# A one-core decoder step: the cached keys of each sample transposed in 32x32 blocks on VectorE and scored by sixteen 32x32 tiles of TensorE

## What is computed

```python
s_past = einsum('nqhd,nkhd->nhqk', q, k_past) * ATTN_SCALE + cq - c_past   # k_past: 2048 x 16 x 64
s_new  = einsum('nqhd,nkhd->nhqk', q, k_new)  * ATTN_SCALE + cq - c_new    # causal among the 4 new rows
p = softmax(concatenate([s_past, s_new]))
out = p[past] @ v_past + p[new] @ v_new
```

## Time and profile before

| what | us |
|---|---|
| median of 3 runs (lowest, highest) | 1737.45 (1736.69, 1746.53) |
| span of the profiled execution | 1738.2 |
| TensorE busy in the span | 1580.9 (91%) |
| one iteration of the attention loop | 62.0 |
| attention, first key transpose to second projection tile | 721.4 to 1250.0 |

### The profile page before, as it was taken

One profiled execution on the slowest core, in us unless ns is written; L12 is line 12 of the kernel. 1 busy time (PEld: TensorE's weight loads), 2 busy tenths in 40 slices (PEclk: granted clock), 3 DMA queues, 4 the chain that ended last, 5 costly groups with the idle time before them and its releaser, 6 DMA issues.

```text
span 1738.2 us, 23311 instructions
## 1 busy us (share of the span) xinstructions
PE 1580.9 (91%) x7920; PEld 864.2 (50%) x7920; DVE 484.5 (28%) x1110; ACT 339.2 (20%) x696; POOL 120.1 (7%) x176
## 2 busy tenths in 40 slices
PE   4999999999849999599999999999995999999992
PEld 4874444444424444265656555555444444444440
DVE  3330000000032232355555554555124100000002
ACT  2120000000111111333333333433210000000010
POOL 1020000000020000100001010010000300000002
PEclk8899999999969999789999999999995999999996
DMA  8279888888871131558988898888623588888755
GB/s 247 105 247 338 330 336 333 334 332 322 300 251 37 49 97 49 189 182 269 300 299 288 288 298 285 297 301 295 246 115 122 153 333 335 334 336 338 321 217 184
DMA packets 115110, 435.78 MB, mean 251 GB/s; under 512 B 26823, under 2 KB 44296, under 8 KB 102511
## 3 DMA queue, kind: packets, MB, share of 16 engines
q1 hardware_dynamic: 85111, 370.75, 59.0%
q0 software_dynamic: 11472, 33.92, 6.1%
q10 hardware_dynamic: 18480, 30.48, 4.8%
HBM read 397.90 MB, written 37.58 MB: 251 GB/s over the span
## 4 chain that ended last, share of the span: by engine, by line
PE 73%; issue 12%; SPq 4%; DVE 3%; DMA 3%; ACT 3%; POOL 1%; ACTq 0%; DVEq 0%; POOLq 0%
PE PS L839 24%; PE PS L857 12%; PE PS L938 10%; PE PS L1079 6%; PE PS L1145 3%; PE PS L1097 3%; PE PS L1063 3%; PE PS L780 3%; PE PS L1024 2%; SPq L460 2%; PE PS L1044 1%; SPq L386 1%; DMA KB<-yd,SLi 1%; PE PS L847 1%; PE PS L1127 1%
## 5 line engine op out<-in xcount | busy, mean ns | idle before, releaser
L839 PE MATMUL PS<-W,VB 128*128 128x512 f32 x1024 | 454.7, 598 | 9.7 <-DVE VB L1572 5.5
L839 PEld LDWEIGHTS PS<-W,VB 128*128 128x128 f32 x1024 | 194.1, 192 | 242.2 <-issue 230.7
L857 PE MATMUL PS<-W,VB 128*128 128x512 f32 x512 | 226.9, 596 | 4.2 <-ACT VB L1295 4.2
L1722 DVE TENSOR_TENSOR VB<-VB,PS 128x512 f32<-128x512 f32 x32 | 22.0, 688 | 617.5 <-PE PS L839 617.5
L1079 PE MATMUL PS<-C,KB 128*128 128x128 f32 x1024 | 167.9, 295 | 12.4 <-ACT W L1458 10.8
L1079 PEld LDWEIGHTS PS<-C,KB 128*128 128x128 f32 x1024 | 117.5, 147 | 78.3 <-issue 59.4
L857 PEld LDWEIGHTS PS<-W,VB 128*128 128x128 f32 x512 | 95.7, 192 | 113.7 <-issue 109.1
L1301 ACT ACTIVATE VB<-PS 128x1024 f32<-128x1024 f32 x32 | 32.7, 1023 | 436.1 <-PE PS L857 436.1
L1458 ACT ACTIVATE W<-PS 128x512 f32<-128x512 f32 x128 | 76.1, 594 | 170.2 <-PE PS L1079 161.6
L1900 DVE COPY W<-PS 128x512 f32<-128x512 f32 x128 | 88.0, 688 | 65.5 <-PE PS L1079 63.7
L1097 PE MATMUL PS<-W 128*32 128x256 f32 x1024 | 84.3, 402 | 2.9 <-DVE W L1995 1.4
(11 more groups left out here) (255 smaller groups left out, 1454.0 us busy)
## 6 DMA issues: line engine op xcount, KB each, us to landing
W<-in_w_gate SPq DMA_DIRECT2D x32, 2048.0 KB, 13.3
W<-in_w_up SPq DMA_DIRECT2D x32, 2048.0 KB, 17.7
W<-in_w_down SPq DMA_DIRECT2D x32, 2048.0 KB, 8.7
KB<-in_cache_k SPq DMA_DIRECT2D x128, 512.0 KB, 5.3
W<-in_cache_v SPq DMA_DIRECT2D x64, 512.0 KB, 5.6
VB<-in_cache_v SPq DMA_DIRECT2D x64, 512.0 KB, 7.3
yd<-VB ACTq DMA_DIRECT2D x32, 512.0 KB, 11.3
W<-in_w_kvf SPq DMA_DIRECT2D x4, 2048.0 KB, 15.7
```

Of the source, the lines that this page charges most:

```text
L839: mm = pe.matmul(PS[:, bank, :], XT[:, k, :], w[:, k, :], start=(k == 0), stop=(k == KC - 1))
L857: mm = pe.matmul(PS[:, 5 + n, :], HT[:, f, :], w[:, f, n * 512:(n + 1) * 512], start=(f == 0), stop=(f == FC - 1))
```

## The change

The transposes leave TensorE. VectorE transposes each page of keys in place, in 32x32 blocks (one instruction of 128x1024 per page, 16 per sample). After that, partition 32a+d of block b of a page holds feature d of that block for the 32 rows 32a to 32a+31. TensorE multiplies 32x32 query tiles with them: for each of 32 blocks, four tiles (row group a, column group c4), 512 columns wide, each row group a into a PSUM bank of its own; 128 products per sample, and eight of them add up in each output. All of a sample's keys must be on the chip for that, so `KB` and `VB` together now hold the 16 pages of one sample, and the values keep two slots of a chunk in `W`. The prompt's weights are copied out of PSUM by ScalarE. The first iteration runs the prompt 12 ticks ahead of the sample. The values' product works by chunks, chunks 2 and 3 of sample i-1 in iteration i. The last sample's chunks 2 and 3 come before the output projection. The added query layout is built once: four products with the gain and one transpose.

```diff
-KTICKS = 32
-SHIFT = 3
-TICKS = KTICKS + 2
-QK_TICK = [2 * x + 3 for x in range(KTICKS // 2)]
-NEW_TICK = 18
-P_TICK = (5, 7, 9, 11, 16)
-O_TICK = [g + 8 for g in range(PAGES + 1)]
-OT_TICK = 27
+SHIFT = 12
+TICKS = V_TICK[-1] + 1
+QK_TICK = (0, 2, 4, 6)
+NEW_TICK = 24
+SCORE_TICK = 8
+EXP_TICK = 10
+HI_TICK = (11, 13)
+OB_TICK = 15
+OT_TICK = 16
+P_TICK = (17, 18, 19, 20, 21)
+LO_TICK = (27, 30)
+K_TICK = tuple(range(10, 18)) + tuple(range(24, 32))
...
-        VSL = [W[:, 4, :], W[:, 5, :], VB[:, 0, :], VB[:, 1, :]]
+        VSL = [W[:, 4, :], W[:, 5, :]]
+        KPG = KV[:, :, :].rearrange("p a (g n) -> p (a g) n", n=D)
...
SyncE:
+            load_chunk(KV[:, 2, :], k_rows, 0, 2, sem("k_in2"))
             sp.wait_ge(sem("qts_ready"), NT)
+            sp.wait_ge(sem("k4_ready"), 1)
+            sp.wait_ge(sem("qt_ready"), 1)
             sp.wait_ge(sem("ktd_out"), 32 * NT)
             sp.wait_ge(sem("qtd_out"), 32 * NT)
...
+            load_chunk(KV[:, 3, :], k_rows, 0, 3, sem("k_in3"))
+            def attention_loads(i, first=False, last=False):
+                if not first:
+                    for ch in (2, 3):
+                        sp.wait_ge(sem("pv_done"), NCH * i - 4 + ch - 1)
+                        load_chunk(VSL[ch - 2], v_rows, i - 1, ch, sem(f"v_in{ch - 2}"))
+                sp.wait_ge(sem("qk_done"), i + 1)
+                for h in range(2):
+                    if last:
...
+                    else:
+                        load_chunk(KV[:, h, :], k_rows, i + 1, h, sem(f"k_in{h}"))
+                if not last:
+                    sp.wait_ge(sem("s_ready"), 4 * i + 4)
+                    load_bias(i + 1)
+                for ch in range(2):
+                    after(sp, sem("pv_done"), NCH * i - 2 + ch + 1)
+                    load_chunk(VSL[ch], v_rows, i, ch, sem(f"v_in{ch}"))
+                if not last:
+                    for h in range(2, 4):
+                        load_chunk(KV[:, h, :], k_rows, i + 1, h, sem(f"k_in{h}"))
TensorE:
+                def qk(part):
+                    if part == 0:
+                        pe.wait_ge(sem("kt_done"), PAGES * (i + 1))
+                        pe.wait_ge(sem("sn_ready"), i + 1)
+                    for j in (2 * part, 2 * part + 1):
+                        for c4 in range(4):
+                            b = 8 * c4 + j
+                            for a in range(4):
+                                rows = slice(32 * a, 32 * a + 32)
+                                mm = pe.matmul(PS[32 * c4:32 * c4 + 32, a, :], QB32[rows, b, :], KPG[rows, :, 32 * b:32 * b + 32],
+                                               start=(j == 0), stop=(j == 7), tile_position=(32 * a, 32 * c4), skip_group_check=True)
...
             pe.wait_ge(sem("pu_ot"), 10 * NB)
+            values(NB - 1, 2)
+            values(NB - 1, 3)
             project_out(0)
-            attention(NB, front=False)
-            pe.wait_ge(sem("s_ready"), NCH * NB)
+            out_transposes(NB - 1)
             project_out(1)
ScalarE:
-                dst = TS if t < 4 else QT4
-                if t < 4:
-                    act.wait_ge(sem("ktd_out"), 32 * (t + 1))
+                dst = TS
+                act.wait_ge(sem("ktd_out"), 32 * (t + 1))
VectorE:
+            def keys_transposed(i, g):
+                if g % CH == 0:
+                    dve.wait_ge(sem(f"k_in{g // CH}"), 64 * (i + 1))
+                dve.transpose(KPG[:, g, :], KPG[:, g, :]).then_inc(sem("kt_done"), 1)
+                def scores():
+                    dve.wait_ge(sem("qk_done"), i + 1)
...
+                    for a in range(4):
+                        dve.tensor_tensor(SV[:, :, a, :], PS[:, a, :].rearrange("p (g n) -> p g n", n=32), BV[:, :, a, :], ALU.add)\
+                            .then_inc(sem("s_ready"), 1)
+                    dve.wait_ge(sem("s_ready"), 4 * i + 4)
+                    dve.tensor_reduce(sst[:, 0:1], SROW[:, :], X, ALU.max, negate=True).then_inc(sem("sp_max"), 1)
                 for n in range(TICKS + shift):
                     m = n - shift
+                    if m == SCORE_TICK:
+                        scores()
+                        if not last:
+                            queries_in(i + 1)
...
+                    if n in S_TICK:
+                        pmax(S_TICK.index(n))
+                    if n - 1 in S_TICK:
+                        pnorm(S_TICK.index(n - 1))
...
+                    if not last and m in K_TICK:
+                        keys_transposed(i + 1, K_TICK.index(m))
+                    if first and n < SHIFT and n % 3 == 2:
+                        for g in range(CH):
+                            keys_transposed(0, CH * (n // 3) + g)
```

More of the change, by code:

```diff
@@ L44 @@
 LINKS = 5 + NT
-SMALL = 20
+SMALL = 21
 NORMS = [("pool", 0)]
@@ L1178, in _ @@
-            attention(0, back=False, shift=SHIFT)
-            with pe.Fori(1, NB) as i:
+                    if m in QK_TICK:
+                        qk(QK_TICK.index(m))
+                    if m == NEW_TICK and not last:
+                        new_keys(i + 1)
+                    if not first and m in HI_TICK:
+                        values(i - 1, 2 + HI_TICK.index(m))
+                    if not first and m == OT_TICK:
+                        out_transposes(i - 1)
+                    if m in P_TICK:
+                        p_transposes(P_TICK.index(m))
@@ L1519, in _ @@
-            attention(0, back=False, shift=SHIFT)
-            with act.Fori(1, NB) as i:
+                    if m == EXP_TICK:
+                        act.wait_ge(sem("sp_max"), i + 1)
+                        act.activation(SROW[:, :], SROW[:, :], ACT.Exp, bias=sst[:, 0:1], accum_out=sst[:, 1:2])\
+                            .then_inc(sem("sp_exp"), 1)
+                    if not first and m == OB_TICK:
+                        out_scaled(i - 1)
+                    if m in P_TICK:
+                        p_out(P_TICK.index(m))
@@ L1886, in _ @@
                     merge(4, "v_mm", 3)
[L1888 to L1900 removed]
+            dve.wait_ge(sem("kn_ready"), 2 * NT)
```

434 lines of the change are left out of this document (181 added, 253 removed).

## The result

The kernel after takes 1782.67 us (median of 4 runs, 1779.49 to 1785.28), the kernel before beside it 1739.54 us (1736.69 to 1746.53): ratio 1.0241, 95% interval 1.0217 to 1.0264, slower. The forecast was 1771 in a range of 1722 to 1850. The profiled execution spans 1780.7 us against 1738.2.

A forecast was written before the change was run, and what follows sets the result against it. TensorE bounded the kernel before; afterwards no engine is full and a 59.0 us ring of transfers sets the loop. 1738.2 + 13.4 = 1751.6, plus 20 of clock, 1771.6, less 0.75: 1771, range 1722 to 1850.

The forecast's parts named there:

- What leaves and joins TensorE: TensorE's load per iteration: 59.4 - 18.6 - 9.1 + 7.3 = 39 us, so it stops being the bound.
- VectorE and ScalarE: Their load per iteration: a page's transpose 1.22 us, VectorE 36.4 us, ScalarE 18; no engine full.
- ring: Loop period from one score block's end to the next, through key loads, last transposes and block: 59.0 us without the clock.
- slow: Rival: VectorE's page transpose takes 2.3 us, a ring is some 68 us, total about 1848; chance 0.08.
- fast transpose: Rival: page transpose 0.75 us and clock holding, ring 56 us, total 1722; chance 0.12 including better overlap.
- The wait that takes over: Loop: next block waits for key page 16 and its transposes; 3.5 + 39.0 + 5.7 + 10.3 + 0.5 = 59.0 us.
- The start: First iteration: VectorE's transposes between prompt units and a 3 us wait for keys; first block ends at 782.8.
- The end: After the last block: 53.4 us before the output projection, second tile at 1263.4, 13.4 us later than before.
- The clock: TensorE's clock falls after idle stretches: 2.5 us a sample (0 to 7.3), 20 us in all.
- The sum: Total without the clock: 1738.2 + 13.4 = 1751.6; the loop wins 21 us, start and end give back 34.
- the clock stays up: Rival: same ring in the loop with TensorE's clock up, total 1751; chance 0.21.
- row groups take turns: Rival: score block's row groups not fully side by side; 1829 if two at a time, 1947 if one; chance 0.16.

The follow-up runs named there:

- e2: Kernel after, with SyncE asking for the next sample's key chunks 2 and 3 ahead of value chunks 0 and 1: 1769.35 us, ratio 1.0184.
- e8: Kernel after, with a semaphore for each page of key chunk 3 and for pages 0 and 1 of chunk 2: 1778.6 us, ratio 1.0205.
- e1_pages: Kernel after, with a semaphore for each of the last four key pages, so VectorE can transpose each once landed: 1777.25 us, ratio 1.0221.
- e4_tail: Kernel after, with the first output projection ahead of the products with the last sample's value chunks 2 and 3: 1777.44 us, ratio 1.0214.
- e6_fill: Kernel after, with unread products filling TensorE's idle time ahead of the last transposes and unit 2's transposes, from sample 1 on: 1807.03 us, ratio 1.0367.

## Why the prediction was right, and where it was not

The sign and the order of causes came out, and the size within 12 us of 1783, of a change of 43 of which 34 were forecast. Step by step:

- **What leaves and joins TensorE.** It stopped being the bound. The block was put at 7.3 us of products, at 29 ns each; it measures 9.1 (4 x 2.28, 36 ns). With the unit steps between the parts a block is 10.9 us at full clock, and the prediction had 10.3. Four column tiles at 512 columns would be 114 ns, so four row groups bring a factor of 3.2, neither 4 nor 1. The figure that the prediction took from the Trainium skill ("TensorE: Matmul & The Clock Gate", Part 3), sixteen tiles at 10.6 times one, would be 11.0 us of products; the trace has 9.1, and the measurement decides. The same table of the Trainium skill gives four row tiles 3.07 times one; the 3.2 of this trace is near it.
- **VectorE and ScalarE.** 1.22 us for a page, 2.32 for the long maximum (2.3 forecast); VectorE is busy 34.9 us a ring (36.4), ScalarE 17.7 (18). The "slow" and the "fast transpose" rivals fall with the first number. By the Trainium skill's estimate, as the prediction quoted it, a page was 1.07 us and a fixed part; the trace's 1.22 leaves 0.15 us for that part.
- **The wait that takes over.** A ring of 59.0 and 2.5 of clock, 61.5 in all; measured 427.9 / 7 = 61.1. Of the parts: keys asked for 0.9 us behind the block (0.9), the last key page landed at 41.7 to 42.5 (42.5), the next block in the ring shown at 49.9 (48.2, or 48.7 with the semaphores' 0.5), the block itself 10.9 to 13.1 but for the first, with 15.8. So the term of the transfers was right. The term behind it was not: the block starts 7.1 to 8.2 us behind the last landing in all rings but the first, where 5.7 and 0.5 were forecast, because VectorE isn't through with chunk 2's pages when chunk 3's are there. This is the step in which the prediction was nevertheless incomplete: it said that no engine is full and so "everything follows from the order of transfers". The runs show that the chain of unit steps through TensorE, VectorE and ScalarE is as long as the chain of transfers, to within 3 us: two megabytes less gave 17 us for 40, keys that landed 7 to 12 us earlier in each ring (e2) gave 10 us in all for 25, waits page by page 3 for 25 and 6 for 15 to 20, one list's stall removed 1 for 25. The forecast called this "a ring with no slack" in which the block waits for page 16; e8's rings of 61.4 us without one wait for a transfer show what it left out, the lists' own length. As a sum for the time it didn't matter, since both chains give 61, and that they do is luck: nothing in the working added up the lists' steps. As advice on what to change it would have failed, and it did in e1_pages.
- **The start.** The prompt's first product was forecast at 740.6, and came at 751.4. The wait for the keys' transfer was put at 3 us, with 7 as its bound; ScalarE waited 11.2. But GpSimd, which needs both transfers, was only 1.5 us later behind the first of them than before (15.4 for 13.9 us): what one transfer waited, the other had waited before. Another 4.1 us came where nothing was forecast: the first head's data took 8.45 us from its issue to the product instead of 4.34, with twelve key pages asked for from 725.73 on, the last four from 743.58, just behind this data; from 743 to 751 the DMA share is 0.82, and it was 0.44 over the same steps before. That the pages are the cause is likely, and not tested. With 1.7 us more on the way to the keys' transfer that is 7.3 us, against 3. A further 6.5 us lay in the projections and what is ahead of them, which the change doesn't touch; in the twelve other variants that point is reached 1.2 us earlier to 11.0 us later than in the one profile of the kernel before, so how much of it belongs to the change stays open. From the first product to the end of the first block: forecast 42.2, measured 42.0. Here two errors cancelled: the block began 26.2 us behind that product for 29.6, and took 15.8 us for 12.6. That is over the 14 us that the prediction gave as a sign of being wrong. Of the 3.2 us, 1.7 lie in its first part, which ran at a clock of 0.50 (4.08 us for 2.35), and 1.8 in the products, at 36 ns for 29; row groups that take turns would have cost at least 7.3.
- **The end.** From the last block to the second projection tile: forecast 53.4 + 14.2 = 67.6, measured 71.0. The 3.4 us lie in units 3 to 9: 37.2 us from unit 2's division to the end of the product with value chunk 1, for 32; before it 7.2 for 8, behind it 12.5 for 13.4. That the projection's cover is lost was right, and e4_tail gives back 5 to 7 us of it.
- **The clock.** Forecast 2.5 us a sample. It shows in the rows at either level: a part of the block takes 2.35 us at full clock and 4.08 at half behind a wait of 6.75 us. All eight blocks together are 11.7 us longer than at full clock (98.9 less 8 x 10.9). Seven rings are 14.9 us longer than the ring without the clock, of which 4.2 are the mis-sized block (7 x 0.6); some 11 are left for the clock and what wasn't seen, against 17.5. In e6_fill, where TensorE didn't idle ahead of the blocks from the third on, each of these took 10.9 us.
- **The sum.** 1263.4 for the second projection tile without the clock, 1292.3 measured: 6.5 in unchanged work, 4.3 at the start, 14.9 in the rings, 3.4 at the end, less 0.2. With the 20 us of clock the forecast was 8.9 us short in the trace, and 12 in the medians; of the 3 us between, most is that the median lies 2.0 us above this span, where the forecast took it 0.75 below, as with the kernel before. The 6.5 us in unchanged work were forecast by nothing, and aren't shown to come from the change.

Most other signs came as named: blocks 59.9 to 62.2 us apart, SyncE's waits in the loop longest for the last score product (125.6 us in eight), the first projection tile at 1278.2, a clock of 0.78 to 0.89 in the loop but 0.72 in its first ring, no ring under 57 us, a DMA share of 0.86 to 0.87.

Of the rivals, "the clock stays up" fell with the block's first parts, "row groups take turns" with 36 ns a product.

## What to carry to other kernels

Work that is taken off the bound is worth only the distance to the next chain, and a chain is not found from busy shares: in a ring where no engine is over 85% busy and transfers at 0.87, two chains of 58 to 61 us lay side by side. In the loop an edit to one of them alone gave at most 17 us; keys first, division first and earlier transposes together, with the two ends put right, gave 53, of which the ends alone had given 25. Before reading "VectorE waits for a transfer" as "the transfers set the pace", take the wait away and look at who waits next. And here single-buffering what was double-buffered moved costs to the two ends of the loop, where they were cheap to win back: transposing what has already landed while the engine waits for something else (20 us) and putting independent work over the last transfers (5 us) gave half of what was won.

## What the runs showed of the hardware

- A 128x1024 block-wise transpose in place on VectorE takes 1.22 us at 32 bits, the same as the 1.22 us of two operands of that size in the earlier trace rows and more than its 0.75 us of one.
- Sixteen 32x32 tiles in 32 bits sustain a 512-column instruction every 36 ns at a granted clock of 1.00 (64 in 2.28 us).
- 64 of 128 rows of a page moved at 201 GB/s with the DMA engines at 0.97, full pages at 410 GB/s at 1.03. The 333 GB/s that the prediction worked out from an iteration's mean is therefore no ceiling of the transfers; it is a mean over full pages, stretches of small pieces and gaps. In the kernel after, full pages move at 1068.7, the forget biases (landing from 1051.7 to 1056.3) at 1052.7, and next to nothing at 1082.7 (columns as in the earlier trace rows):

```profile
1052.70:1054.70 2.00, 2.00 (x18) 0.81 (x10) 0.00 (x0) 0.60 (x1) 0.00 (x0) 1.00 0.95 137
1068.70:1070.70 2.00, 1.40 (x7) 0.93 (x7) 0.51 (x2) 0.68 (x2) 0.00 (x0) 1.00 1.05 422
1082.70:1084.70 2.00, 2.00 (x33) 0.97 (x25) 2.00 (x3) 0.00 (x0) 0.00 (x0) 0.95 0.01 4
```

- The same unchanged stage ahead of the attention was reached at 677.1 us in the kernel before and at 675.9 to 688.1 us in the executions of thirteen changed kernels; what makes the spread isn't known.
